# The tail of a hybrid mixer: two score groups moved between value products, one norm ahead of another, and a weight panel's split moved

## The reference, cut to what matters

```
h  = rms_norm(x, mix_norm_pre[l]) * (1 + sc_m) + sh_m          # 256 tokens x 1024
cq, k, v, k_idx, w_idx, q_m, k_m, v_m, o_m, i_m, f_m = split(h @ w_in)
att = softmax(q k^T / 8 + mask) @ v                            # 8 heads of 64
att = rms_norm(att, attn_out_norm)                             # per head
hm  = mlstm(q_m, k_m, v_m, i_m, log_sigmoid(f_m))              # 4 heads of 128
hm  = sigmoid(o_m) * rms_norm(hm, mlstm_out_norm)              # per head
y   = concatenate([att, hm]) @ w_out                           # output linear
x   = x + g_m * rms_norm(y, mix_norm_post[l])
```

## Time and profile before

| | before |
|---|---|
| device time, median of 3 runs | 2208.17 us (2204.88 to 2209.29) |
| the profiled execution's own time | 2208.01 us |
| its span | 2206.2 us |
| PE busy | 2022.4 us (92%) |
| DVE busy | 1506.3 us (68%) |
| ACT busy | 901.2 us (41%) |
| mean granted PE clock | 0.951 |

### The profile page before, as it was taken

The page is one execution under the profiler, slowest core; times in us unless marked ns, Lnnn a source line. Parts: engine busy times, 40 slices in busy tenths (PEclk is TensorE's granted clock), DMA queues, the critical chain, the costliest instruction groups (busy, mean ns, idle before and its releaser), DMA issues. The chain is left out here.

```text
span 2206.2 us, 39921 instructions
## 1 busy us (share of the span) xinstructions
PE 2022.4 (92%) x16746; PEld 1799.7 (82%) x16746; DVE 1506.3 (68%) x2318; ACT 901.2 (41%) x1336; POOL 140.4 (6%) x231
## 2 busy tenths in 40 slices
PE   5998988999999799799988999798799989989997
PEld 4786765788888578688886999788699979878997
DVE  6866556898676768656646777778766666856454
ACT  3436443222222442322325444556444455544443
POOL 0100000010100011201210000000000000000000
PEclk7999989999999899999998999899899989988999
DMA  8532022455543266000004787343368734323552
GB/s 329 198 134 77 1 92 99 155 200 179 209 171 134 81 238 229 30 3 3 3 22 153 254 275 274 120 148 112 118 212 282 276 107 172 115 96 115 189 177 91
DMA packets 59132, 323.92 MB, mean 147 GB/s; under 512 B 6384, under 2 KB 7536, under 8 KB 32624
## 3 DMA queue, kind: packets, MB, share of 16 engines
q1 hardware_dynamic: 33360, 228.97, 29.4%
q0 software_dynamic: 25344, 92.29, 11.9%
q10 hardware_dynamic: 288, 0.66, 0.1%
HBM read 320.84 MB, written 1.05 MB: 146 GB/s over the span
## 5 line engine op out<-in xcount | busy, mean ns | idle before, releaser
L370 DVE TENSOR_TENSOR w_low<-raw,w_high 128x1024 fp32r<-128x1024 f32 (+1 forms) x408 | 473.2, 1201 | 231.8 <-ACT w_high L362 231.5
L362 ACT ACTIVATE w_high<-raw 128x1024 fp32r<-128x1024 f32 (+1 forms) x408 | 402.3, 1034 | 400.0 <-PE banks L407 391.2
L548 DVE SCALAR_TENSOR_TENSOR mod_rows<-mod_rows,silu_condition 128x1024 f32<-128x1024 f32 x176 | 212.9, 1221 | 10.3 <-DMA mod_rows<-rows_dram 7.7
L405 PE MATMUL banks<-ffn_a_l,w_high 128*128 128x256 f32 x704 | 199.6, 284 | 1.9 <-DVE ffn_hidden L1023 1.9
L406 PE MATMUL banks<-ffn_a_h,w_high 128*128 128x256 f32 x704 | 199.0, 283 | 0.0
L407 PE MATMUL banks<-ffn_a_h,w_low 128*128 128x256 f32 x704 | 199.0, 283 | 0.0
L405 PE MATMUL banks<-mlp_a_l,w_high 128*128 128x512 f32 (+1 forms) x512 | 176.8, 345 | 11.9 <-DVE mlp_a_l L690 7.7
L534 POOL DMA_DIRECT2D mod_rows<-rows_dram x176 | 93.2, 530 | 1352.8 <-DVE mod_rows L548 1135.5
L406 PE MATMUL banks<-mlp_a_h,w_high 128*128 128x512 f32 (+1 forms) x512 | 175.2, 342 | 0.0
L407 PE MATMUL banks<-mlp_a_h,w_low 128*128 128x512 f32 (+1 forms) x512 | 174.9, 342 | 0.0
L405 PE MATMUL banks<-mlp_hidden_l,w_high 128*128 128x512 f32 (+1 forms) x512 | 173.2, 338 | 1.3 <-DVE mlp_hidden_l L1031 1.3
(11 more groups left out here) (595 smaller groups left out, 4764.6 us busy)
## 6 DMA issues: line engine op xcount, KB each, us to landing
raw<-panels_dram SPq DMA_DIRECT2D x204, 1024.0 KB, 4.8
mod_rows<-rows_dram POOLq DMA_DIRECT2D x176, 512.0 KB, 5.2
mod_0a_rows<-rows_dram SPq DMA_DIRECT2D x8, 1024.0 KB, 20.1
x_features<-x_features_dram SPq DMA_DIRECT2D x1, 2048.0 KB, 11.1
constants<-small_dram SPq DMA_DIRECT2D x1, 1672.5 KB, 6.6
silu_condition<-conditions_dram SPq DMA_DIRECT2D x2, 512.0 KB, 12.3
out_dram<-x_features SPq DMA_DIRECT2D x4, 256.0 KB, 2.1
constants<-small_dram SPq DMA_DIRECT2D x1, 736.5 KB, 5.4
```

The source lines that it names most:

```text
L362: self.nc.scalar.activation(self.wh[:, m % 2, cols], self.raw[:, slot, cols], ACT.Copy).then_inc(self.w_high, 1)
L370: self.nc.vector.tensor_tensor(self.wl[:, m % 2, cols], self.raw[:, slot, cols], self.wh[:, m % 2, cols].bitcast(F32), ALU.subtract).then_ ...
L405: self.nc.tensor.matmul(out, sh(k), ml(k), start=(opens and k == 0), stop=False)
L548: nc.vector.scalar_tensor_tensor(row if v == nv - 1 else self.scratch[:], row, 1.0, self.cond[v][:], ALU.mult, ALU.mult, accum_out=mod[:, ...
```

## The change

Four edits, in both calls alike.

1. The attention scores of groups 1 and 2 are issued on PE ahead of block q = 3 of `mix_vm_in`, behind block 2, instead of behind block 3. ACT's exponentials of group 1 follow its evacuation of block 2 (through `behind`) instead of standing in the tail.
2. In the tail PE makes both parts of the mLSTM values, one behind the other, ahead of the values of group 0. ACT squares both ahead of the exponentials of group 2; the copy-out of group 1 and the squares of the first attention part change places.
3. The mLSTM norm (sums, root, factor, scaling) comes ahead of `att_sums(0)` and `att_scaled(0)` on DVE, and its root ahead of the first attention root on ACT.
4. ACT splits the second panel of `mix_out` in two halves, around the second attention squares (`split_half` with `ahead=1`). DVE's split of it is taken out of the tail, and so is made by `linear` at the head of `mix_out`, behind the low parts.

```diff
--- before.py
+++ after.py
@@ -376,9 +376,9 @@
             (self.split_act if which == "act" else self.split_dve)(eng, self.split_next[which])
             self.split_next[which] += 1
 
-    def split_half(self, act, h):
-
-        m = self.m
+    def split_half(self, act, h, ahead=0):
+
+        m = self.m + ahead
         assert self.split_next["act"] == m
         self.split_act(act, m, parts=(h,))
         self.split_next["act"] += h
@@ -2955,8 +2955,25 @@
             pr.split_upto("act", eng, pr.m)
             probs(eng, 0)
 
-    pr.linear("mix_vm_in", 2, 2, 4, pr.tokens(high, low, 2, PC, KD), vals(vm), [], engines=("act",),
-              banks=(0, 1), prior=b_info, info=vm_info, beside=beside_last, carry=False)
+    value_tokens = pr.tokens(high, low, 2, PC, KD)
+
+    def values_and_scores(q, m, bank):
+        if q == 3:
+            nc.tensor.wait_ge(ml_scored, 8)
+            scores(nc.tensor, 1)
+            nc.tensor.wait_ge(logits_out, 1)
+            scores(nc.tensor, 2)
+        return value_tokens(q, m, bank)
+
+    values_out = [0]
+
+    def probs_behind(which, eng):
+        values_out[0] += 1
+        if values_out[0] == 3:
+            probs(eng, 1)
+
+    pr.linear("mix_vm_in", 2, 2, 4, values_and_scores, vals(vm), [], engines=("act",),
+              banks=(0, 1), prior=b_info, info=vm_info, beside=beside_last, carry=False, behind=probs_behind)
 
     @pr.block.tensor
     def _(pe):
@@ -2986,25 +3003,20 @@
                                             vm[:, j, h * P:(h + 1) * P], start=(j == 0), stop=(j == i))
             last.then_inc(m_done, 1)
 
-        pe.wait_ge(ml_scored, 8)
-        scores(pe, 1)
-        pe.wait_ge(logits_out, 1)
-        scores(pe, 2)
-        for q in range(4):
-            pe.wait_ge(*vm_info["taken"][q])
+        pe.wait_ge(*vm_info["taken"][2])
         for b, i, j in ((bank_turn[0], 0, 0), (bank_turn[1], 1, 0), (bank_turn[2], 1, 1)):
             for h in range(MH):
                 last = nc.tensor.transpose(ps[:, b, h * P:(h + 1) * P], S[:, i, h, j * P:(j + 1) * P], c("ident"))
             last.then_inc(m_t_done, 1)
         pe.wait_ge(logits_out, 2)
         turn_probs(0)
+        pe.wait_ge(*vm_info["taken"][3])
         ml_values(0)
-        pe.wait_ge(m_t_out, 2)
-        values(0, bank_o[0])
+        ml_values(1)
         pe.wait_ge(logits_out, 3)
         turn_probs(1)
+        values(0, bank_o[0])
         turn_probs(2)
-        ml_values(1)
         values(1, bank_o[1])
         values(2, bank_o[1])
         for i in range(2):
@@ -3037,19 +3049,19 @@
             act.wait_ge(m_t_done, g + 1)
             nc.scalar.activation(St[g], ps[:, b, :], ACT.Copy).then_inc(m_t_out, 1)
         probs_out(0)
-        probs(act, 1)
+        for i in range(2):
+            squares(m_squared, (m_done, i + 1), hm_sq[:, i, :], bank_m[i])
         probs(act, 2)
-        squares(m_squared, (m_done, 1), hm_sq[:, 0, :], bank_m[0])
+        probs_out(1)
         squares(o_squared, (o_done, 1), att_sq[:, 0, :], bank_o[0])
-        probs_out(1)
         probs_out(2)
+        act.wait_ge(m_summed, 1)
+        nc.scalar.activation(ml_root, ml_t, ACT.Sqrt, bias=c("eps")).then_inc(m_rooted, 1)
         act.wait_ge(o_summed, 1)
         nc.scalar.activation(root_a[:, 0], t2[:, 0], ACT.Sqrt, bias=c("eps")).then_inc(o_rooted, 1)
-        squares(m_squared, (m_done, 2), hm_sq[:, 1, :], bank_m[1])
-        pr.split_upto("act", act, pr.m + 1)
-        act.wait_ge(m_summed, 1)
-        nc.scalar.activation(ml_root, ml_t, ACT.Sqrt, bias=c("eps")).then_inc(m_rooted, 1)
+        pr.split_half(act, 0, 1)
         squares(o_squared, (o_done, 2), att_sq[:, 1, :], bank_o[1])
+        pr.split_half(act, 1, 1)
         act.wait_ge(o_summed, 2)
         nc.scalar.activation(root_a[:, 1], t2[:, 1], ACT.Sqrt, bias=c("eps")).then_inc(o_rooted, 1)
         for b in range(4):
@@ -3096,11 +3108,10 @@
         ch.then(dve, nc.vector.tensor_tensor(den, den, em, ALU.max))
         ch.then(dve, nc.vector.reciprocal(inv, den))
         pr.split_upto("dve", dve, pr.m)
-        att_sums(0)
-        att_scaled(0)
         dve.wait_ge(m_squared, 2)
         ch.then(dve, nc.vector.tensor_reduce(ml_ss, hm_sq.rearrange("p i (h n) -> p i h n", n=P), AX.X, ALU.add))
         scale(ml_ss, inv, ml_t, ML_D, m_summed)
+        att_sums(0)
         dve.wait_ge(m_rooted, 1)
         ch.then(dve, nc.vector.reciprocal(ml_root, ml_root))
         ch.then(dve, nc.vector.tensor_tensor(ml_f, ml_root, inv, ALU.mult))
@@ -3108,7 +3119,7 @@
             nc.vector.tensor_tensor(hm[:, i, :].rearrange("p (h n) -> p h n", n=P),
                                     ps[:, bank_m[i], :].rearrange("p (h n) -> p h n", n=P),
                                     spread(ml_f[:, i], 2, P), ALU.mult).then_inc(m_scaled, 1)
-        pr.split_upto("dve", dve, pr.m + 1)
+        att_scaled(0)
         dve.wait_ge(om_sigmoid, 1)
         att_sums(1)
         gate_ml((0, 1))
```

## The result

The changed kernel takes 2193.33 us (median of 5 runs, 2188.90 to 2195.15) beside 2208.02 us for the kernel before: a ratio of 0.9928 (95% interval 0.9914 to 0.9941). Measured again twice it took 2196.93 and 2194.98 us, ratios 0.9947 (0.9927 to 0.9968) and 0.9945 (0.9931 to 0.9959). So it is faster, by 12 to 15 us (under 1%); I had forecast 9.4 and a range that ends at 2193.5. The profiled execution took 2193.6 us.

The account below looks back on a forecast made before the run. PE was busy 92% of the span, so only its waits in two alike tails could give time. Each tail was to save 4.65 us, 2.27 of it the split: 9.3 off 2208.0, forecast 2198.8 us, range 2193.5 to 2204.

Parts of the forecast that it names:

- The scores ahead of block 3: PE's scores swapped with block 3: logits of group 1 start at 27.0 instead of 29.88, the copies 0.6 us later.
- The switch: PE going between dense products and scores: taken as 0, with bounds of 0 to 0.3 us.
- The mLSTM values together: Tail, PE and ACT: second values done at 35.95 with 0.5 us to spare, second square from 36.0 to 36.5.
- The mLSTM norm first: Tail, DVE: the second attention sums are reached at 45.2 instead of 49.85, 4.65 us earlier.
- second table load: Rival on ACT: exponentials reload their table behind the squares, 5.1 us over both tails, 2203.9 us; chance 0.03.
- The moved split: DVE's second-panel split gives 2.27 of the 4.65 us, hidden behind the linear's first panel with 1.2 us to spare.
- The later load of a panel: SP's queue: the panel three further on loads 4.3 us later, wanted some 15 us on, so costs nothing.
- I take the clock as unchanged: Output linears' heads: the low clock stays as before; bounds are 4.2 us gained and 2.6 lost.
- The sum: Both tails together: twice 4.65 us is 9.3 us saved.
- The rival with 0.12, 4.2 us: Output linears: the clock never falls or is back when the linear starts, 4.2 us less, 2194.6 us; chance 0.12.
- Its bound: Low clock at the two linears' heads: at most 1.65 and 2.55 us lost, 4.2 together.
- the other bound: Output linears' heads: low clock for 6.8 us in both, an estimate, 2.6 us lost.

Follow-up runs that it names:

- the filled kernels: The kernels before and after, each with products of the identity by itself put into PE's waits in the tail: 2205.04 us and 2194.01 us.
- a variant with the old wait: The kernel before with one edit alone, DVE's split of the second output panel moved out of the tail: 2203.30 us (0.9977).
- one with a longer wait: The kernel after with the norms back in the old order on DVE and ACT's two roots swapped back: 2203.76 us (0.9972).
- an experiment where one queue was left out: The kernel after with DVE's low parts of the first two mLSTM blocks ahead of the last gating: 2201.49 us (0.9962).
- before_warm: The kernel before with 11, 9 and 2 products of the identity by itself in PE's tail waits: 2205.04 us (0.9984).

## Why the prediction was wrong

- **The scores ahead of block 3: right.** Logits of group 1 were to start 3.6 us ahead of the transposes and did 3.65 (19.07, 22.72). The switch, taken at 0 to 0.3, cost 0.07 a tail.
- **The mLSTM values together: right, 0.3 us too small.** The second square was to start 5.4 us behind the transposes and did 5.07. Most of it: I had PE's twelve transposes end where its wait began, 1.53 us on; without that wait the next group starts after 1.31 (24.03 - 22.72). From that square to the table load I had 4.85 and it was 4.87.
- **The mLSTM norm first: right.** Second sums 14.6 us behind the transposes forecast, 14.24 measured; the difference is the one above. No second table load came, as the row of the square had said, and not as a reading of the list of shared functions in the Trainium skill ("ScalarE: Activation LUTs", the section on table sets) would have it.
- **The moved split: right.** It starts 2.35 us behind the first product (2.4 forecast), PE doesn't wait for it, and undone it costs 2.27. The later load of a panel cost nothing either: with the clock full the linears take 23.3 us in both kernels. With the scores (1.24) and the norms (2.1) undone singly, the three edits that were undone carry what their queues said.
- **"I take the clock as unchanged": this step failed.** The sum was 9.3; the queues gave 9.84. The other 3.5 us stand where the clock differs: 1.4 and 0.8 at the linears' heads, 0.6 and 0.7 behind them. For the heads the filled kernels show it; for the rest only the records of the clock do. I had put this term at nothing, reasoning that a stretch with only transposes would do the same as before though a third shorter. It didn't: the low level at the heads lasted 3.2 and 5.1 us before, none and 3.2 after. Why it fell that way I can't say: PE's wait ahead of the mLSTM transposes went from 2.86 to 1.07 us, but a variant with the old wait and one with a longer wait also had a full first head. The rival with 0.12, 4.2 us, was near in size partly by luck: it had the whole gain at the heads with none of it low, where the heads gave 2.25 us, the second stayed low for 3.2, and 1.3 came from behind them, which I had not looked at. Its bound held: I allowed at most 1.65 and 2.55 us for the two heads, and they had cost 1.4 and 2.25. (The 6.8 us of the other bound should be 6.9 by its own rows.) The range's lower end should have reached that rival whole (2194.6 less what the queues may be off), not cut it at its edge. By the measured median the miss past the range is 0.2 us; the two further medians of after lie in it. What is beyond doubt is the 13.4 against 9.3 between the profiles.

## What to carry to other kernels

Lay out each engine's queue from the rows of one profile: the tail of the whole change came out within 0.4 us that way and those of five variants within 0.2, and in an experiment where one queue was left out the linear behind the tail went wrong. Put a range for the clock beside that sum, from what the low level costs in the rows: here it gave a third more, and in variants with tails between the two it gave other amounts in no order that I could lay out beforehand. Compare profiles by stretches between fixed marks: the total hid in 5 us of chance what the stretches showed to 0.1 us.

## What the hardware showed that I had not expected

- What the low clock costs at the linears repeated to 0.1 us in executions whose tails began up to 4 us apart (23.30 and 24.7 us for the linears in three executions of the kernel after), and changed with each edit: L-E between 23.3 and 24.8 in the first linear, 23.3 and 25.5 in the second, for the same 192 products. Yet in the first tail of after one execution of three has a low stretch ahead of the linear and two have none.
- 22 products by the identity, put into PE's waits, held the clock at 1.00 through a tail and delayed nothing in it (before_warm: T-L unchanged, 2205.04 us against 2208.54). In the kernel after, two thirds of the gain at the head were given back further on: E-end grew by 0.9 us, with 21.5 us at the low level instead of 18.5.
- The same code ahead of the tails took 1517.6 to 1530.8 us over 14 profiles, with 136.5 to 163.8 us of it at the low level. Between profiles of one kernel without filling in the norms this stretch is nearly all of the difference in the total.
